# FFN tiles in narrow passes alone, and h laid 128 bytes further on

## The reference, cut to what matters

```python
for i in range(DEPTH):                       # 4
    x = x + 0.5 * _swiglu(_rms_norm(x, norm_ffn1[i]), ffn1_w_gate[i], ffn1_w_up[i], ffn1_w_down[i])
    x = x + mixer_i(_rms_norm(x, norm_mix[i]))
    x = x + 0.5 * _swiglu(_rms_norm(x, norm_ffn2[i]), ffn2_w_gate[i], ffn2_w_up[i], ffn2_w_down[i])

def _swiglu(h, w_gate, w_up, w_down):        # 1024 -> 2816 -> 1024
    return (jax.nn.silu(h @ w_gate) * (h @ w_up)) @ w_down
```

## Time and profile before

| | |
|---|---|
| median of three runs | 1986.03 us (1985.21 to 1986.44) |
| span of the profiled execution | 1984.6 us |
| PE busy | 1955.5 us (99%), 12574 instructions |
| PEld busy | 1717.6 us (87%) |
| DVE busy | 1420.7 us (72%) |
| ACT busy | 1044.4 us (53%) |
| wide passes, on x and on h | 2816 and 1408 |
| bytes moved by DMA | 350.14 MB, mean 176 GB/s |

### The profile page before, as it was taken

One profiled execution on the slowest core, in us unless ns is written; L12 is line 12 of the kernel. 1 busy time (PEld: TensorE's weight loads), 2 busy tenths in 40 slices (PEclk: granted clock), 3 DMA queues, 4 the chain that ended last, 5 costly groups with the idle time before them and its releaser, 6 DMA issues.

```text
span 1984.6 us, 29082 instructions
## 1 busy us (share of the span) xinstructions
PE 1955.5 (99%) x12574; PEld 1717.6 (87%) x12574; DVE 1420.7 (72%) x1645; ACT 1044.4 (53%) x1250; POOL 101.6 (5%) x114
## 2 busy tenths in 40 slices
PE   7999999999999998999999999999999999999999
PEld 6888889888888896988888888788888888888887
DVE  7776678875787565877587658887758765778763
ACT  6554566554555344654465455575436544566542
POOL 3000001000200001100100000010000000001000
PEclk9999999999999998999999999999999999999999
DMA  7655434655665683665656553356566655435653
GB/s 238 194 183 182 149 128 154 192 188 189 192 191 180 201 249 83 191 191 182 200 191 192 177 184 128 107 176 191 183 196 190 191 183 180 148 128 171 191 189 107
DMA packets 336365, 350.14 MB, mean 176 GB/s; under 512 B 10077, under 2 KB 331886, under 8 KB 336238
## 3 DMA queue, kind: packets, MB, share of 16 engines
q1 hardware_dynamic: 331742, 343.58, 54.1%
q10 hardware_dynamic: 4496, 4.70, 1.2%
HBM read 346.04 MB, written 2.22 MB: 175 GB/s over the span
## 4 chain that ended last, share of the span: by engine, by line
PE 94%; DVE 3%; ACT 2%; issue 1%; POOL 1%; DMA 0%; ACTq 0%; DVEq 0%; POOLq 0%
PE banks L1443 49%; PE banks L1448 24%; PE banks L1434 5%; PE banks L1436 5%; PE banks L1435 5%; PE banks L1901 1%; PE banks L1660 1%; PE banks L1713 1%; ACT sb_w_high L470 1%; DVE sb_w_low L808 1%; PE banks L1680 1%; PE banks L1697 1%; ACT sb_scores L598 0%; PE banks L1818 0%; PE banks L1667 0%
## 5 line engine op out<-in xcount | busy, mean ns | idle before, releaser
L808 DVE TENSOR_TENSOR sb_w_low<-sb_raw,sb_w_high 128x2048 fp32r<-128x2048 f32 (+1 forms) x332 | 749.5, 2262 | 208.8 <-ACT sb_w_high L470 208.2
L1443 PE MATMUL banks<-sb_x_both,sb_w_high 128*128 128x512 f32 x2816 | 721.9, 393 | 1.9 <-ACT sb_w_high L470 1.9
L470 ACT ACTIVATE sb_w_high<-sb_raw 128x2048 fp32r<-128x2048 f32 (+1 forms) x332 | 618.5, 1867 | 122.2 <-DMA sb_raw<-in_ffn_w_down 109.0
L1443 PEld LDWEIGHTS banks<-sb_x_both,sb_w_high 128*128 128x128 f32 x2816 | 500.2, 189 | 82.2 <-ACT sb_w_high L470 2.3
L1448 PEld LDWEIGHTS banks<-sb_x_both,sb_w_low 128*128 128x128 f32 x2792 | 386.5, 188 | 35.2
L1448 PE MATMUL banks<-sb_x_both,sb_w_low 128*128 128x256 f32 x2792 | 394.6, 279 | 0.0
L1443 PE MATMUL banks<-sb_h_both,sb_w_high 128*128 128x512 f32 x1408 | 360.2, 395 | 0.0
L1443 PEld LDWEIGHTS banks<-sb_h_both,sb_w_high 128*128 128x128 f32 x1408 | 250.8, 188 | 45.3
L1448 PEld LDWEIGHTS banks<-sb_h_both,sb_w_low 128*128 128x128 f32 x1408 | 190.9, 188 | 16.9
L1448 PE MATMUL banks<-sb_h_both,sb_w_low 128*128 128x256 f32 x1408 | 194.4, 279 | 0.0
L488 ACT ACTIVATE sb_x_both<-sb_xT,sb_vec 128x256 fp32r<-128x256 f32 x96 | 43.3, 501 | 200.8 <-DVE sb_xT L841 176.1
(11 more groups left out here) (229 smaller groups left out, 1936.6 us busy)
## 6 DMA issues: line engine op xcount, KB each, us to landing
sb_raw<-in_ffn_w_gate SPq DMA_DIRECT2D x88, 1024.0 KB, 5.4
sb_raw<-in_ffn_w_up SPq DMA_DIRECT2D x88, 1024.0 KB, 5.3
sb_raw<-in_ffn_w_down SPq DMA_DIRECT2D x64, 1024.0 KB, 5.0
sb_raw<-in_ffn_w_down SPq DMA_DIRECT2D x32, 768.0 KB, 4.3
sb_raw<-in_fox_w_in SPq DMA_DIRECT2D x24, 1024.0 KB, 5.2
sb_raw<-in_conv_w_pw SPq DMA_DIRECT2D x12, 1024.0 KB, 5.4
sb_raw<-in_diff_w_in SPq DMA_DIRECT2D x12, 1024.0 KB, 5.0
sb_raw<-in_fox_w_out SPq DMA_DIRECT2D x8, 1024.0 KB, 4.8
```

The lines of the kernel that those rows point to most:

```text
L470: act.activation(slot(w_high, b)[:, 0:width(b)], slot(raw, b)[:, 0:width(b)], ACT.Copy).then_inc(S["high_ready"], 1)
L808: dve.tensor_tensor(slot(w_low, b)[:, 0:width(b)], slot(raw, b)[:, 0:width(b)], slot(w_high, b)[:, 0:width(b)].bitcast(F32), ALU.subtract) ...
L1443: return pe.matmul(pair(bank[at][:, :]), high[:, n * P:(n + 1) * P], m_both, start=first, stop=last, skip_group_check=True)
```

## The change: what it does

Tiles of pairs 1 to 10 and all tiles of the down projection go through a new function, `few_wide`, with `wide` 0. For each k it issues high weights by the high half and high weights by the low half as two narrow passes (`on_part`), each with its own load of the same weights; after all k come the narrow passes of the low weights, the last of which ends the group. With `wide` above 0 the first so many k would have wide passes as before; no caller asks for that. The first pair keeps `both_parts`. `shift_h` grows from 200 to 232 values, so `h_both` and what is declared after it lie 32 x 4 = 128 bytes further on.

```diff
-        sb("shift_h", [P, 200])
+        sb("shift_h", [P, 232])
...
+            def on_part(at, n, high, m_part, half, first, last):
+
+                return pe.matmul(bank[at][:, half * SEQ:(half + 1) * SEQ], high[:, n * P:(n + 1) * P], m_part,
+                                 start=first, stop=last, skip_group_check=True)
+
+            def few_wide(at, n, high, low, m_both, ks, first, last, wide):
+
+                for k in ks[:wide]:
+                    on_both(at, n, high[:, k, :], m_both(k), first and k == ks[0], False)
+                for k in ks[wide:]:
+                    for half in range(2):
+                        on_part(at, n, high[:, k, :], m_both(k)[:, half, :], half,
+                                first and k == ks[0] and half == 0, False)
+                for k in ks[:-1]:
+                    on_high(at, n, low[:, k, :], m_both(k)[:, 0, :])
+                k = ks[-1]
+                return pe.matmul(bank[at][:, SEQ:2 * SEQ], low[:, k, n * P:(n + 1) * P], m_both(k)[:, 0, :],
+                                 start=False, stop=last, skip_group_check=True)
...
-                def tile(which, p, n, ks):
+                def tile(which, p, n, ks, wide=None):
...
+                    if wide is not None:
+                        return few_wide(pair_banks(p) + 2 * which + n, n, high, low, lambda k: x_both[:, :, k, :],
+                                        list(ks), ks[0] == 0, ks[-1] == KT - 1, wide)
...
-                            ins = tile(which, p, n, range(KT))
+                            ins = tile(which, p, n, range(KT), 0)
...
-                        ins = both_parts(2 * (T % 2) + n, n, high, low, lambda k: h_both[:, :, first + k, :],
-                                         list(range(last - first)), c == 0, c == len(DOWN) - 1)
+                        ins = few_wide(2 * (T % 2) + n, n, high, low, lambda k: h_both[:, :, first + k, :],
+                                       list(range(last - first)), c == 0, c == len(DOWN) - 1, 0)
```

## The result

The changed kernel takes 2021.1 us, median of four runs (2019.1 to 2022.9), where the kernel before, run beside it, takes 1985.6: a ratio of 1.0169 (95% interval 1.0157 to 1.0181). By the ratio it is slower by some 34 us. Forecast were 2015 us in a range from 1960 to 2019: the right way and nearly the right size, with the median 2 us above the range.

A forecast was written before the change was run, and what follows sets the result against it. TensorE's pass pace was taken to bound the kernel. The profiled 1984.6 us plus 29.3 for slow-paced FFN passes, with other terms at 0, and 1.4 around the span gave 2015 us; range 1960 to 2019.

The forecast's parts named there:

- Bound and counting: TensorE in the FFNs: busy 99% of the span, time set by pass pace; 3968 of 4224 steps change.
- Which pace: Narrow runs behind each FFN's sum of squares enter at the slow 117.8 ns and keep it: +29.3 us over eight FFNs.
- the one analogue in the trace: Convolution's input projection behind its sum of squares, 699.76 to 739.10: 334 distances at 117.8 ns, taken as evidence for slow entry.
- All fast: Rival for the FFN passes: entry is fast or the slow state decays, 113.4 ns, -22.9 us, 1963 us; chance 0.29.
- h 128 bytes on: Down projection: the shift puts h where x is, so down inherits gate and up's pace; slow, 62.2 instead of 61.3 us.
- the term for all that lies outside the changed passes: Attention output's 768 passes, moved by the shift: priced 0, bounds 3.4 us either way; order and waits priced at nothing.
- The likeliest case: Changed FFN passes slow throughout: 2015 us, alone 2009 to 2019 with attention +-4; chance 0.53.
- The bound for this: Attention output's 768 passes: 3.4 us dearer or cheaper if all changed pace by 4.4 ns.
- The one stretch that the prediction followed: Attention output passes, 302.30 to 305.93: leave the slow pace after a few, then 31 distances at 113.2 ns.
- The prediction's clock of 0.997: Matmul engine's granted clock over the span, read as the 2.4 GHz level from end to end.

The follow-up runs named there:

- x_further_on: The changed kernel with shift_x 48 for 16, so x_both and h_both lie 192 instead of 64 bytes past a multiple of 1024 from the weights; 1967.0 us.
- all_narrow_o: The changed kernel with shift_x 48, the first pair's pieces narrow (all but the very first pair) and shift_o 88 for 24; 1962.3 us, ratio 0.988.
- passes_alone: The changed kernel with shift_h back at 200: narrow passes, h and the mixers' tensors at their old places; 2016.4 us, ratio 1.0147.
- shift_alone: The kernel before with shift_h 232 for 200 alone, wide and narrow passes as before; 1985.9 us, ratio 0.9994.
- first_tile_1_wide: The changed kernel with one wide pass at the head of the first tile behind each sum of squares; 2020.3 us, ratio 1.016.
- first_tile_3_wide: The changed kernel with three wide passes at the head of the first tile behind each sum of squares; 2020.6 us, ratio 1.0165.

## Why the prediction was right or wrong

*Bound and counting*: right. The time went where the paces put it; all eight gate and up stretches grew by 2.74 to 2.80 us (forecast 2.77), and down by 0.88 where it is in one piece (forecast 0.89).

*Which pace*: right, from the one analogue in the trace, the convolution's projection. The experiments make the state more than an analogy: entry sets it, and at x's old place nothing in gate and up unsets it. That the forecast entry was the slow one rests on one stretch, and it held.

*"All fast"* was the right rival at the right price: 1963 us was worked out for it, and x_further_on, whose profile has seven of eight FFNs fast, takes 1967.0. That all_narrow_o takes 1962.3 is in part luck: it has the first pairs narrow and the convolution's projection at the fast pace as well (38.39 us instead of 39.85), which that sum didn't hold. What turns it on is the entry or the place, not a decay at the place as it was.

*h 128 bytes on*: the state does pass from gate and up to down, as forecast. But it passes at the old place of h too (passes_alone), so my reason, that the shift puts h where x is, wasn't needed there. It was needed in the first and the last FFN, behind the fp32 work in down: at the old place those passes turn fast, 3.0 us in all, and the prediction has no word on them.

*The step that failed* is the term for all that lies outside the changed passes. The likeliest case took it as 0, with 4 us either way for attention and nothing for the first blocks, and so set the range's top at 2019. In the profiled execution the span grew by 32.7 us, of which the changed passes are 8 x (2.77 + 0.88) = 29.2. The other 3.5 us, read from the starts of the sums of squares and of the FFNs:

- The first blocks of the four mixers run at the slow pace: 206.55 to 212.09 for 47 distances, 117.9 ns, where the earlier trace rows had 113.4. Four times 0.2, 0.8 us. The prediction used those blocks as evidence of the fast pace and didn't ask what they would be entered from. In shift_alone they are at 117.8 too, without the new passes.
- From the sum of squares of an attention phase with a forget gate to that of the next FFN, 132.03 us (212.21 to 344.24) instead of 131.25 in phase 2, 0.78, and 0.94 more in phase 11: 1.7 us. Output projections, at the slow pace throughout, are 0.4 of it in each; the rest is in passes with x. shift_alone has the same 0.78 and 0.94, passes_alone 0.18 and 0.40, so most of it is the shift's. The bound for this was in the text, the value taken was 0. The one stretch that the prediction followed wasn't typical: in the kernel before, some 100 of 180 such distances in phase 2 are at the fast pace, and none in the convolution.
- Up to the first sum of squares, 29.16 instead of 28.17: 1.0 us. It is the landing of a small first load, `in_norm_ffn`, by which TensorE begins at 8.07 instead of 7.07. In the chain of waits, first the kernel before, then the changed one:

```profile
1.66 5.27 DMA sb_wide<-in_norm_ffn
...
1.68 6.26 DMA sb_wide<-in_norm_ffn
```

TensorE's clock isn't the cause: it is done with the first pair early and waits 2.47 us for the sum of squares from GpSimd. The rows of its timeline for the three terms, in the changed kernel:

```profile
206.55 0.28 PE L1434 MATMUL banks<-sb_x_both,sb_w_high 128*128 128x256 f32 x1
...
212.09 0.28 PE L1436 MATMUL banks<-sb_x_both,sb_w_low 128*128 128x256 f32 x1
212.21 0.60 PE L1517 MATMUL banks<-sb_square_sum,sb_ones 128*128 128x256 f32 x2
...
29.16 0.70 PE L1517 MATMUL banks<-sb_square_sum,sb_ones 128*128 128x256 f32 x2 [2.47 <-POOL sb_square_sum L407]
```

TensorE's first pass starts at 6.94 to 7.07 us in the three profiles of kernels with the old passes and at 7.35 to 8.07 in the ten others: part of the third term may come with the change, part is scatter, and why the load lands later isn't shown. A smaller slip: what lies around the span is 1.8 us in the executions of either kernel (2019.14 against 2017.3 here), not 1.4.

The profiled execution took 2019.1 us; the other three took 2019.7, 2022.5 and 2022.9, with a mean granted clock of 0.995 where they were longest. Those executions have no profile, but a kernel of nearly the same passes shows where it can happen: the convolution's phase, from its sum of squares to the next, takes 115.92 us in the changed kernel and 118.28 in first_tile_1_wide. There TensorE waits and its clock falls to the 1.2 GHz level for stretches, more of them in the second row, first_tile_1_wide:

```profile
755.00:805.00 50.00, 41.82 (x569) 28.58 (x560) 28.40 (x38) 22.63 (x35) 11.36 (x4) 0.90 0.39 94
755.00:805.00 50.00, 41.34 (x544) 27.45 (x537) 29.35 (x38) 22.53 (x35) 9.20 (x4) 0.86 0.36 83
```

(The prediction's clock of 0.997 "from end to end" is a mean that hides such stretches.) So the mechanism was right, and the term beside the changed passes was mis-sized: 0 where the mixers cost 2.5 us and the start 1.0, with a range that left little room for scatter between executions. That the median came out above 2019, and not just below, is in part chance.

## What to carry to other kernels

Where TensorE never waits, read the distance between starts, not the duration, and look whether the same instruction has more than one distance before pricing a change by its mean. If it has, ask what each stretch is entered from and whether anything resets it: taking out an instruction of another kind can take out the reset, and moving an operand by some bytes can bring it back. Try place and pass shape together, since the best place for the one was the worse for the other here.

## What the runs showed of the hardware that I had not expected

A stream of narrow fp32r passes, each with its own weight load, has two steady paces, 113.3 and 117.8 ns, kept for more than a thousand passes. Where the streamed operand lies at 64, one wide pass in the settled round brings the first on (113.6 ns from the next pass), an fp32 matmul the second (118.1 ns over 348 passes behind it). With h 64 bytes before a multiple of 1024, the passes behind the same fp32 matmuls are at 113 or 114 from the sixth distance on.

128 bytes in the place of x, and of all that is declared behind it, change 852 into 885 passes per 100 us of gate and up, with code, weights' place and PSUM banks unchanged. The Trainium skill, "SBUF — State Buffer", section "Who interferes with whom", gives TensorE two independent read ports, for the streamed operand and for the weights, and says that it never waits on anyone. From independent ports alone one wouldn't expect the place of the streamed operand to matter; the stretches of x_further_on and the changed kernel, 885 against 852, show that it does. Why is open.

The clock at the start differs between the profiles. In the one of first_tile_3_wide TensorE waits 3.28 us for the first sum of squares, and the next passes run at the 1.2 GHz level, a granted clock of 0.50 from 29 to 32:

```profile
28.68 1.22 PE L1517 MATMUL banks<-sb_square_sum,sb_ones 128*128 128x256 f32 x2 [3.28 <-POOL sb_square_sum L407]
29.34 1.84 PE L1443 MATMUL banks<-sb_x_both,sb_w_high 128*128 128x512 f32 x3
30.98 1.85 PE L1464 MATMUL banks<-sb_x_both,sb_w_high 128*128 128x256 f32 x10
```

Ten narrow passes take 1.69 us there instead of 1.18. In the profile of the changed kernel, where that wait is 2.47 us, the 5 us from 25 to 30 have a granted clock of 1.00.
